# Products of a normed x: high and low part of x in one matmul of 512 columns, with an eviction in two steps

## What is computed

```
x = x + hybrid_mixer(x)        # rmsnorm(x) @ w_in -> gated delta rule and attention, @ w_out
x = x + cross_attention(x)     # rmsnorm(x) @ w_xq, rmsnorm(mem) @ w_xkv, @ w_xo
x = x + conv_ffn(x)            # silu(conv(h @ w_gate)) * (h @ w_up) @ w_down
x = rmsnorm(x)
x = layernorm(ALPHA * x + mamba2(x))                  # x @ a_w_in -> conv, state space scan, @ a_w_out
x = layernorm(ALPHA * x + window_attention(x))        # x @ kv_w, x @ b_w_in, @ b_w_out
```

## Time and profile before

| | us |
|---|---|
| median of 3 runs | 2474.08 |
| lowest and highest run | 2471.7 and 2499.8 |
| span of the profiled execution, first to last instruction | 2471.0 |
| PE busy, weight loads busy | 2434.6, 2376.3 |
| DVE busy | 1727.8 |
| ACT busy | 1220.4 |

### The profile page before, as it was taken

How to read it: one execution, slowest core, us unless ns; L and a number is a source line. 1 busy time by engine, 2 the same in 40 slices (tenths; PEclk the granted TensorE clock), 3 DMA queues, 4 the chain that set the end, 5 groups by cost and what they waited for, 6 DMA issues and landing times.

```text
span 2471.0 us, 51530 instructions
## 1 busy us (share of the span) xinstructions
PE 2434.6 (99%) x20866; PEld 2376.3 (96%) x20866; DVE 1727.8 (70%) x2768; ACT 1220.4 (49%) x1918; POOL 437.7 (18%) x535
## 2 busy tenths in 40 slices
PE   7999999999999999999999999999999999999998
PEld 7999999999999999999999999999999999899998
DVE  6677646685666656665657877777787778777777
ACT  5434334554544444444444545444445554566554
POOL 1233310160200000000003201330101112511002
PEclk9999999999999999999999999999999999999999
DMA  6433335565455556556556654454454445444453
GB/s 220 158 124 120 127 126 180 189 200 171 155 196 193 193 176 212 197 176 212 195 174 190 195 167 157 161 179 156 156 189 153 158 158 183 151 154 144 149 163 118
DMA packets 124501, 418.34 MB, mean 169 GB/s; under 512 B 13796, under 2 KB 17644, under 8 KB 124012
## 3 DMA queue, kind: packets, MB, share of 16 engines
q1 hardware_dynamic: 124268, 415.06, 51.1%
HBM read 412.37 MB, written 3.68 MB: 168 GB/s over the span
## 4 chain that ended last, share of the span: by engine, by line
PE 93%; DVE 3%; POOL 2%; issue 1%; ACT 1%; DMA 0%; SPq 0%; ACTq 0%; POOLq 0%; DVEq 0%
PE b L766 27%; PE b L767 27%; PE b L768 27%; PE b L744 2%; PE b L1109 1%; DVE WL L1647 1%; PE b L887 1%; DVE t1s L1745 1%; PE b L900 1%; PE b L1120 1%; PE b L737 1%; POOL t1s L2547 0%; PE b L1175 0%; POOL ACC L2378 0%; PE b L1214 0%
## 5 line engine op out<-in xcount | busy, mean ns | idle before, releaser
L766 PE MATMUL b<-XH,WH 128*128 128x256 f32 x4224 | 1196.5, 283 | 18.2 <-DVE WL L1647 14.6
L768 PE MATMUL b<-XH,WL 128*128 128x256 f32 x4224 | 1173.5, 278 | 0.0
L767 PE MATMUL b<-XL,WH 128*128 128x256 f32 x4224 | 1173.4, 278 | 0.0
L1236 ACT ACTIVATE WH<-WR 128x1024 fp32r<-128x1024 f32 (+2 forms) x811 | 817.6, 1012 | 505.0 <-PE b L768 500.3
L1647 DVE TENSOR_TENSOR WL<-WR,WH 128x1024 fp32r<-128x1024 f32 (+2 forms) x811 | 984.5, 1223 | 14.9 <-ACT WH L1236 14.7
L766 PEld LDWEIGHTS b<-XH,WH 128*128 128x128 f32 x4224 | 795.7, 188 | 30.4 <-issue 14.2
L767 PEld LDWEIGHTS b<-XL,WH 128*128 128x128 f32 x4224 | 795.8, 188 | 3.0 <-issue 2.4
L768 PEld LDWEIGHTS b<-XH,WL 128*128 128x128 f32 x4224 | 797.0, 189 | 0.0
L766 PE MATMUL b<-OH,WH 128*128 128x256 f32 x1680 | 472.9, 282 | 2.9 <-DVE WL L1647 2.4
L768 PE MATMUL b<-OH,WL 128*128 128x256 f32 x1680 | 466.6, 278 | 0.0
L767 PE MATMUL b<-OL,WH 128*128 128x256 f32 x1680 | 466.5, 278 | 0.0
(11 more groups left out here) (397 smaller groups left out, 2241.5 us busy)
## 6 DMA issues: line engine op xcount, KB each, us to landing
WR<-a_w_in SPq DMA_DIRECT2D x160, 512.0 KB, 3.7
WR<-w_in SPq DMA_DIRECT2D x112, 512.0 KB, 3.6
WR<-w_gate SPq DMA_DIRECT2D x88, 512.0 KB, 3.8
WR<-w_up SPq DMA_DIRECT2D x88, 512.0 KB, 4.2
WR<-a_w_out SPq DMA_DIRECT2D x64, 512.0 KB, 3.5
WR<-b_w_in SPq DMA_DIRECT2D x64, 512.0 KB, 3.5
WR<-w_down SPq DMA_DIRECT2D x64, 384.0 KB, 3.5
WR<-w_down SPq DMA_DIRECT2D x64, 320.0 KB, 2.9
```

The lines of the kernel that those rows point to most:

```text
L766: mm(ps, WH[:, slot, at:at + P], xh, start=(k == 0), stop=False)
L767: mm(ps, WH[:, slot, at:at + P], xl, start=False, stop=False)
L768: m = mm(ps, WL[:, slot, at:at + P], xh, start=False, stop=(k == p["kt"] - 1))
L1236: act.activation(WH[:, s, 0:n], WR[:, r, 0:n], ACT.Copy).then_inc(*act_w.up(i))
```

## The change

1. `XH` and `XL` become two halves of one tensor `X2`, `OH` and `OL` of one tensor `O2`, so that an access of shape 128 x 2 x 256 covers the high and the low part of a block.
2. For every product that isn't of kind res or pair (`wide`), `half_of` issues two matmuls per block in place of three: one of 512 columns with the high weights over both parts of x, into the whole bank (first half wh xh, second half wh xl), and one of 256 columns with the low weights over the high part, added into the second half.
3. Such a product lies in two halves of a bank and these have to be added. ACT copies the second half into the place in SBUF (`low_half`, with the bias where there is one), then DVE adds the first half of the bank to it in place, and then, as before, multiplies, this time from SBUF. For bkv and swq the sum is all that is left for DVE.
4. Kind swg: ACT's tanh reads the summed gate from SBUF, and DVE's joining of the tanh and the gate (`swa_gate`) is a step of its own that stands later in the plan.

The core of the diff (waits on a place to come free, which `low_half` takes over for each kind, are left out here):

```diff
@@ Plan.evac
+        if p["evac"] == "swg":
+            self.lows.append(("swgate", key[1]))
@@ tensors
-    XH = sb("XH", [P, 16, S], F32R)
-    XL = sb("XL", [P, 16, S], F32R)
-    OH = sb("OH", [P, 16, S], F32R)
-    OL = sb("OL", [P, 16, S], F32R)
+    X2 = sb("X2", [P, 2, 16, S], F32R)
+    O2 = sb("O2", [P, 2, 16, S], F32R)
+    XH, XL, OH, OL = X2[:, 0, :, :], X2[:, 1, :, :], O2[:, 0, :, :], O2[:, 1, :, :]
@@ half_of (PE)
+                if wide(p):
+                    full = banks[p["bank"]][:, :]
+                    mm(h2(full), WH[:, slot, at:at + P], both, start=(k == 0), stop=False)
+                    m = mm(full[:, S:2 * S], WL[:, slot, at:at + P], xh, start=False, stop=(k == p["kt"] - 1))
+                    continue
                 mm(ps, WH[:, slot, at:at + P], xh, start=(k == 0), stop=False)
                 mm(ps, WH[:, slot, at:at + P], xl, start=False, stop=False)
                 m = mm(ps, WL[:, slot, at:at + P], xh, start=False, stop=(k == p["kt"] - 1))
@@ ACT
+        def low_half(key, p):
+            lo = banks[p["bank"]][:, half(1)]
+            kind, i, bias = p["evac"], key[1], None
+            w.wait_ge(*pe_prod.of(key))
...
+            if bias is None:
+                act.activation(to, lo, ACT.Copy).then_inc(*act_ev.up(key))
+            else:
+                act.activation(to, lo, ACT.Identity, bias=bias).then_inc(*act_ev.up(key))
+
         def evac(key):
             v = version(key)
+            p = plan.products[key]
+            if p["evac"] not in ("res", "pair"):
+                low_half(key, p)
...
             if key[0] == "wg":
                 ti = key[1]
-                w.wait_ge(*pe_prod.of(key))
+                w.wait_ge(*dve_ev.of(key))
                 if ti:
-                    w.wait_ge(*dve_ev.of(("wg", ti - 1)))
-                act.activation(T1(8), banks[plan.products[key]["bank"]][:, 0:S], ACT.Tanh, scale=0.5).then_inc(
-                    *act_swa.up("th", ti))
+                    w.wait_ge(*dve_swa.of("g", ti - 1))
+                act.activation(T1(8), T1(ti % 4), ACT.Tanh, scale=0.5).then_inc(*act_swa.up("th", ti))
@@ DVE, evac
-            ps = banks[p["bank"]][:, 0:S]
+            ps, lo = (banks[p["bank"]][:, half(j)] for j in range(2))
+            def whole(to):
+                w.wait_ge(*act_ev.of(key))
+                dve.tensor_tensor(to, to, ps, ALU.add).then_inc(*dve_ev.up("sum", key))
+                w.wait_ge(*dve_ev.of("sum", key))
+                return to
...
             if kind == "conv":
                 w.wait_ge(*dve_norm.of("rb", p["src"]))
-                dve.tensor_tensor(cvs[:, p["c"] % 3, p["K"] - 1:p["K"] - 1 + S], ps, RB[:, :], ALU.mult).then_inc(
-                    *dve_ev.up(key))
+                to = whole(cvs[:, p["c"] % 3, p["K"] - 1:p["K"] - 1 + S])
+                dve.tensor_tensor(to, to, RB[:, :], ALU.mult).then_inc(*dve_ev.up(key))
...
             elif kind == "up":
-                dve.scalar_tensor_tensor(gt[:, 0:S], ps, 0.5, gt[:, S:2 * S], ALU.mult, ALU.mult).then_inc(
-                    *dve_ev.up(key))
+                to = whole(gt[:, 0:S])
+                dve.scalar_tensor_tensor(to, to, 0.5, gt[:, S:2 * S], ALU.mult, ALU.mult).then_inc(*dve_ev.up(key))
...
             elif kind == "swq":
-                dve.tensor_scalar(T1(4 + ti % 2), ps, pc("q_b", ti), None, ALU.add).then_inc(*dve_ev.up(key))
+                w.wait_ge(*act_ev.of(key))
+                dve.tensor_tensor(T1(4 + ti % 2), T1(4 + ti % 2), ps, ALU.add).then_inc(*dve_ev.up(key))
...
+        def swa_gate(ti):
+            w.wait_ge(*act_swa.of("th", ti))
+            dve.scalar_tensor_tensor(T1(ti % 4), T1(8), 1.0, T1(ti % 4), ALU.add, ALU.mult).then_inc(
+                *dve_swa.up("g", ti))
```

More of the change, by code:

```diff
@@ L686, in os_place, with wide @@
                 "up": (i // 11 % 2) * 11 + i % 11, "ssm": i % 16, "swa": i}[stage]
+    def wide(p):
+        return p["evac"] not in ("res", "pair")
     def moving(key, k):
@@ L757, in half_of @@
             for k in range(k0, k1):
-                xh, xl, by = moving(key, k)
+                xh, xl, both, by = moving(key, k)
                 if by[0] == "x":
@@ L1471, in two @@
             x_high(2, m + 1)
+        def low_half(key, p):
+            lo = banks[p["bank"]][:, half(1)]
+            kind, i, bias = p["evac"], key[1], None
+            w.wait_ge(*pe_prod.of(key))
+            if kind == "conv":
+                to = cvs[:, p["c"] % 3, p["K"] - 1:p["K"] - 1 + S]
+                if p["c"] > 2:
+                    w.wait_ge(*dve_cv.of("taps", conv_keys[p["c"] - 3]))
+            elif kind == "gate":
+                to = T1(p["n"] % 2)
+                if p["n"] > 1:
+                    w.wait_ge(*dve_cv.of("n", p["n"] - 2))
+            elif kind == "plain":
+                to = T2(SETS[i % 2]["qkv".index(key[0][1])])[:, half(key[2])]
+                if i == 0:
+                    w.wait_ge(*pe_gdn.of("nr", 2))
+                    w.wait_ge(*dve_os.of("gdn", 5))
+                elif i == 1:
+                    w.wait_ge(*pool_gdn.of("qd", 3))
+                    w.wait_ge(*(pe_gdn.of("xx", 3) if key[0] == "mv" else pe_gdn.of("qk", 3)))
+                else:
+                    w.wait_ge(*(pe_att.of("ns", i - 2) if key[0] == "mv" else pe_att.of("o", i - 2)))
+            elif kind == "kv":
+                to = KM[:, i, :] if i < 4 else T1(7 + i % 2)
+                if i > 5:
+                    w.wait_ge(*pe_kv.of("x", i - 2))
+                elif i > 3:
+                    w.wait_ge(*pe_mem.of("tok"))
+            elif kind == "xq":
+                to = T1(i)
+                w.wait_ge(*dve_os.of("mem", 15))
+            elif kind == "up":
+                to = T2(i % 4)[:, 0:S]
+                w.wait_ge(*pool_up.of(i))
+            elif kind == "bkv":
+                to, bias = T1(i), pc("kv_b", i)
+                w.wait_ge(*pe_ln.of("cols", 0))
+            elif kind == "swg":
+                to = T1(i % 4)
+                if i < 4:
+                    w.wait_ge(*ld_kd[3].of(1))
+                    w.wait_ge(*pool_swa.of("k", 1))
+                else:
+                    w.wait_ge(*dve_os.of("swa", i - 4))
+            else:
+                to, bias = T1(4 + i % 2), pc("q_b", i)
+                if i > 1:
+                    w.wait_ge(*pool_swa.of("q2", i - 2))
+                    w.wait_ge(*pe_swa.of("rope", i - 2))
+            if bias is None:
+                act.activation(to, lo, ACT.Copy).then_inc(*act_ev.up(key))
+            else:
+                act.activation(to, lo, ACT.Identity, bias=bias).then_inc(*act_ev.up(key))
@@ L1808, in evac @@
                     w.wait_ge(*(pe_att.of("ns", pr - 2) if name == "mv" else pe_att.of("o", pr - 2)))
-                to = T2(SETS[pr % 2]["qkv".index(name[1])])[:, half(key[2])]
-                dve.tensor_tensor(to, ps, RB[:, :], ALU.mult).then_inc(*dve_ev.up(key))
+                to = whole(T2(SETS[pr % 2]["qkv".index(name[1])])[:, half(key[2])])
+                dve.tensor_tensor(to, to, RB[:, :], ALU.mult).then_inc(*dve_ev.up(key))
             elif kind == "res":
@@ L1839, in evac @@
                 if m < 4:
-                    dve.tensor_tensor(KM[:, m, :], ps, T1(6), ALU.mult).then_inc(*dve_ev.up(key))
+                    to = whole(KM[:, m, :])
                 else:
@@ L1843, in evac @@
                         w.wait_ge(*pe_kv.of("x", m - 2))
-                    dve.tensor_tensor(T1(7 + m % 2), ps, T1(6), ALU.mult).then_inc(*dve_ev.up(key))
+                    to = whole(T1(7 + m % 2))
+                dve.tensor_tensor(to, to, T1(6), ALU.mult).then_inc(*dve_ev.up(key))
             elif kind == "xq":
@@ L1847, in evac @@
                 w.wait_ge(*act_os.of("mem", 15))
-                dve.tensor_tensor(T1(key[1]), ps, RB[:, :], ALU.mult).then_inc(*dve_ev.up(key))
+                to = whole(T1(key[1]))
+                dve.tensor_tensor(to, to, RB[:, :], ALU.mult).then_inc(*dve_ev.up(key))
             elif kind == "up":
```

25 lines of the change are left out of this document (15 added, 10 removed).

## The result

The changed kernel takes 2528.5 us (median of 4 runs, 2528.3 to 2529.0) where the kernel before takes 2471.7 to 2499.8 in the same comparison: ratio 1.021, 95% interval [1.016, 1.026]. It is slower, by 1.6 to 2.6%; I had forecast 2448 and a range up to 2484. The profiled executions have spans of 2526.7 and 2471.0 us, so 55.7 us are to be found.

The account below looks back on a forecast made before the run. PE's own matmul stream was taken to bound the kernel. Span 2471.0 - 36.6 (matmuls) + 10 (waits) = 2444.4; with the median 3.1 us above the span, 2447.5, rounded to 2448 us; range 2420 to 2484.

Parts of the forecast that it names:

- the price of the matmuls: Wide products on PE: one matmul fewer per block saves a fixed 8.4 ns, x 4352 blocks = 36.6 us.
- the lower one: Lower bound of the matmul saving on PE: surplus follows columns, 512 cost two distances, 0 us saved.
- 10 us of waits: PE waiting for later evictions by ACT and DVE, mostly in the state space part: 10 us added, bounds 0 and 65.
- short loads at 113.3 ns: L784 matmuls with 16 weight columns, still 113.3 ns apart: taken to show the weight load isn't what lengthens a matmul.
- plain f32 streams: Loads beside 512 plain f32 columns start 0.43 us apart: about 2 ns surplus, basis of the upper bound on matmul saving.
- B: Rival on PE's matmuls: surplus follows the columns, a block 339 rather than 340 ns; 2476 us, no change; chance 0.28.
- C: Rival on PE's matmuls: a long stream hides all but 2 ns; 2418 to 2433 us; chance 0.13.
- D: Rival: DVE becomes the bound in the state space part, 0.81 us on each of 80 products; 2502 us; chance 0.09.
- PE's waits on `WL`: Sign: PE's waits on DVE grow from 17 to about 27 us, between 1380 and 1440; above 50 means DVE bounds.
- Blocks: Sign in the feed-forward part: starts of two blocks 333 ns apart if the fixed price per matmul holds.
- Duration of the long matmul: Sign on PE: the 512-column matmul lasts 276 + 107 = 383 ns if the fixed price per matmul holds.
- Two feed-forward products: Sign in the feed-forward part: two products, 10.9 us before, should come in 10.65 us.

Follow-up runs that it names:

- e3: The changed kernel with three matmuls of 256 columns per block again, the eviction in two steps kept: 2483.9 us, ratio 1.005 to the kernel before.
- e2: The changed kernel with the high and low part of a block side by side in SBUF, 1 KB apart in place of 16 KB: 2527.4 us, ratio 1.021.

## Why the prediction was wrong

*The step that failed* is the price of the matmuls: "Taken: the surplus is a fixed price per matmul", 8.4 ns saved on each of 4352 blocks. Measured: 9.5 ns lost on each (353.0 against 343.5). The surplus of 6.6 or 11.2 ns over 106.7 is no property of one matmul. It is a pace (235 ns at 512 is 2 x 117.5) that the place of the operands sets, and that lasts from block to block. At 192 bytes it goes with the columns; at 0 bytes the pair took 346.7 or 353.3 and three matmuls 360, so neither a price per matmul nor one per column covers both places. The two values in the earlier trace rows were the sign of it. I read them as two sizes of one fixed price and carried their mixture over; the question to ask was what chooses between them, and whether the change would choose anew. The mixture itself was mis-sized as well: the mean distance of 343.5 puts 26% of the blocks at the slow pace, not 39%.

*The bound that failed* is the lower one: "512 cost two distances, nothing is saved: 0 us". It assumed that the other matmuls keep their pace. With a mixture of 340 and 353.7 in the rows, the lower bound was a kernel all at the slow one: 4352 x (353.7 - 345.3 by the prediction's own 39%) = 37 us lost, and with the residual products 52. That, with 10 us of waits, is 2536 on the same footing and would have held the result. No unknown mechanism was needed for it, only the rows.

*The evidence that misled*: the earlier trace rows, short loads at 113.3 ns. They show that a short load doesn't improve on the quick pace at this place. They don't show that the load is no part of the surplus: at 0 bytes short loads, in matmuls that put out 16 partitions, took 20 ns off a block. Likewise: plain f32 streams, starts 430 ns apart, did not carry over to fp32r.

*The rivals.* B (the surplus follows the columns) is the nearest: it had the law of this place, no gain from a matmul less, and was wrong by 14 ns per block, since it took the quick pace for the 512 columns. C (all but 2 ns hidden) is out: 227.5 was the best 512 alone. D, my case for slower, is out: PE's waits on `WL` are 17.7 us and not above 50. So the slower side was given to the wrong mechanism, and with 0.03 far too little.

*The list of what would show it.* Blocks: 333 forecast, 353.3 measured. Duration of the long matmul: 383, measured 397. Two feed-forward products: 10.65, measured 32 x 353.3 = 11.3 us. These three say together, without any experiment, that the matmul step is wrong and by how much. ACT's copies: 390 forecast, 381 measured. PE's waits on `WL`: about 27 us and between 1380 and 1440 us forecast, measured 17.7 and none there. So the 10 us put for the waits had the right size and partly the wrong places. DVE's busy time: 1834, measured 1843; the multiplication that now reads SBUF is unchanged in the median (425 ns, L1872), but 14 of 116 were held up beside POOL, which I had not foreseen. Waits and evictions in sum: 10, and 12 by e3.

*The two blocks 16 KB apart* cost nothing, as said (e2: 2527.4).

*The kernel before spreads, the changed one doesn't.* In the comparisons most runs of the kernel before are at 2468 to 2475 and a few at 2497 to 2501; the changed kernel stays within 0.7 us. A pace that is drawn anew in each run from 340 and 353 at 192 bytes would do that: the feed-forward stretch alone, 2,099 blocks at one pace, is worth 2,099 x 13.3 ns = 28 us (an estimate from the table above), and the two groups lie 25 to 30 us apart. The same distance stands between one of e3's ten runs (2510.7) and the others. No trace of a run near 2500 was taken, so this is argued only.

## What to carry to other kernels

Before a change to a stream of matmuls is priced, read the distances of starts and count how many values one shape takes: if there are two, the gap between them, times all the matmuls, belongs into the range as a loss, and whoever claims a gain must say which of the two the new form gets. When a matmul form is compared in a small kernel, put the tensors at the same bytes as in the full one, or try several: here the same pair wins 7 to 13.6 ns a block at 0 bytes and loses up to 13.3 at 192. And average over several starts: one draw can hold for 2,099 blocks. A tensor of a few bytes that nothing reads may be worth 90 us, so keep it in place when tensors are merged, and sweep it when the stream's shape changes.

## What the runs showed that I had not expected

- fp32r matmuls of 256 columns start 113.3, 117.8 or 120 ns apart at the full granted clock, by where the moving tensor stands (0, 64, 128, 160, 192 bytes past 1 KB and more), with weights at a multiple of 1 KB: 2562 against 2472 us for the full kernel.
- A pace persists over products: in the kernel before it never changed within an unbroken stretch, of 2,099 blocks the longest. Unchanged matmuls went from duration 276 to 281 behind wide blocks at 192 bytes, and back to 276 with the wide blocks at 0 bytes.
- Matmuls of 16 weight columns ran at 340 ns per block at 0 bytes where those of 128 took 360; at 192 bytes both showed 340 and 353.
- A DVE multiplication of 128x256 with both inputs in SBUF took 425 ns, but 814 to 1450 beside a `TENSOR_TENSOR` of POOL (14 of 116); with one input in PSUM never over 426, beside POOL or not.
- What stays open: the mechanism behind the places, and what chooses between the two paces when a stream starts or passes to a tensor at another place.
